# A fused layer on one core: the output projection takes the first 128 tokens' four blocks first, and two weight blocks are read twice

## The chip, the cores and the metric

The kernel runs on one core of a Trainium2 chip, in fp32. The number that counts is the device time of one execution, in microseconds. The core's engines are TensorE (PE, with the weight load beside it, PEld), VectorE (DVE), ScalarE (ACT), GpSimd (POOL) and SyncE (SP). SP and POOL issue nearly all transfers; these run on 16 DMA engines, where SP's lie in queue q1 and POOL's in queue q0.

## What is computed

One layer over 256 latent tokens of width 2048. A mixing sub-layer (Fourier groups and an SSD scan, 2048 channels together) is projected by `w_out`, normalised and added to the stream. Then comes an expert retrieval: each token scores 8 heads of keys, picks 16 experts a head, takes a dot of its row with each expert's row of `expert_u`, and adds the rows of `expert_v`, weighted by the results.

```python
y_x = jnp.concatenate([fourier_branch(...), y_x_ssm], axis=-1) @ w_out[layer]   # (256, 2048) @ (2048, 2048)
x = x + gm_x * rms_norm(y_x, g_post_mix[layer])
hx2 = modulate(rms_norm(x, g_pre_ffn[layer]), sf_x, cf_x)
# peer_ffn, for each token t of a block of 128:
q = (tb @ w_query).reshape(tbn, PEER_HEADS, PEER_KEY_DIM)     # 8 heads of 128
s1, s2 = (the halves of q) . sub_keys_1, sub_keys_2           # 128 + 128 scores a head
v1, i1 = top_k(s1, 16); v2, i2 = top_k(s2, 16)                # then top 16 of the 256 sums
act = gelu(einsum('td,thkd->thk', tb, expert_u[idx]))
out = einsum('thk,thkd->td', gate * act, expert_v[idx])
x = x + gf_x * rms_norm(out, g_post_ffn[layer])
```

## The kernel before

The 256 tokens are two tiles of 128, t = 0 and t = 1. A tile and a head are a unit, u = 8 t + h, so there are 16 units of 16 dots each; a dot number n is 16 u + j.

**Weights.** `RING` is the list of the wide weight blocks (2048 x 512, 4.19 MB each), which go in turn through two SBUF slots (`wring`). `ring_load(j)` on SP waits until the block two places earlier has been used (for the projection, by the count `wo_ps` of finished blocks) and issues four pieces of 1 MB. Entries 7 to 10 are the four column blocks of `w_out` (n = 0 to 3), entries 11 and 12 the two of `w_query`.

**Output projection.** `w_out(n, t, ...)` makes one block of the result: 16 products 128x512 into one PSUM bank, `(n % 2) * 2 + t`. `OUT_ORDER` sets the order: (0,0), (0,1), (1,0), (1,1), (2,0), (3,0), (2,1), (3,1). A block whose bank was used before waits for the evacuation by ACT (`wo_out`, count `wo_evac`), and ACT begins with these only after `tail_used` says that all late tiles are done. Late tiles (`late_tiles`) are products on DVE of the modulation vector with rows of `w_mod`, which POOL loads in 512 KB pieces into five slots; `column_sums` adds them up on PE.

**To the dots.** With all four blocks of a tile, DVE makes the new stream row (`x1_make(t)`: two passes over 128x2048), ACT squares it (`x1_norm`), and DVE makes the normalised row (`h2_make(t)`: two passes more). PE transposes it (`h2_transposes`), makes a unit's query (`query(u)`: 16 products of 128x128) and its scores (`key_scores(u)`). ACT copies these out (`q_out`, `scores_out`). DVE routes the unit: `pick_keys(u)` finds the 16 best of each half, `pick_pairs(u)` the 16 best sums and the expert indices (`idx_ready`). POOL gathers by them 128 rows of 8 KB at a time (`gather`, 1.05 MB), and DVE makes the dot (`dot(n)`).

**Slots.** The weight slots become gather slots (`uslot`, 8 of them) only when all 16 queries are done (`q_ps`). Until then the first `U_EARLY` = 20 dots go through five slots (`early`), of which the fifth is the buffer `Grow[1]`, free when `h2_make(1)` is done. In DVE's order, `x1_make(1)`, the routing of unit 0 and `h2_make(1)` stand ahead of dot 0; unit 1 is routed in halves after dots 4 and 9, unit 2 after dots 17 and 21, and so on every 12 or 13 dots. From dot 20 on (`V_POS`) half rows of `expert_v` are gathered between the dots' rows, 62 of them up to dot 130, and PE adds them up with diagonal matrices.

## Time and profile before

| | us |
|---|---|
| median of 3 runs | 1838.02 (1836.51 to 1843.12) |
| the profiled execution | 1832.72 |
| its span | 1830.9 |
| PE, DVE busy | 1457.1, 1311.3 |
| POOL, ACT busy | 891.4, 435.1 |

The profile's times are counted from the start of its span; 1.8 us of the profiled execution lie outside it. In a timeline, consecutive instructions of one kind are merged (x is their number; a product is recorded twice, so 32 are one block of the projection). In the table of windows, each engine's busy time stands with its number of instructions, and then the clock that was granted to TensorE (1.00 is 2.4 GHz, 0.50 is 1.2 GHz), the busy share of the 16 DMA engines and the bytes that they moved. In the rows of the queues, packets and MB are those that were moved inside the window. Matmul ends are modelled, and spans on POOL are rough.

### The profile page before, as it was taken

The page shows a single profiled execution, that of the slowest core. Times are in us where ns is not written, and L with a number is a line of the kernel's source. Part 1 is how long each engine was busy: PE and PEld are TensorE (multiplying, and loading weights), DVE is VectorE, ACT ScalarE, POOL GpSimd, SP SyncE. Part 2 cuts the span into 40 slices and gives each one's busy share as a digit, 9 for nine tenths or more (in the row PEclk, how much of TensorE's full clock was granted, in tenths as well). Part 3 has the DMA queues.
Part 4 walks back from the last instruction along what each step waited for, and adds up shares of the span by engine and source line. Part 5 has one row for each costly group of instructions (what it writes and reads, how often), then busy time and mean ns, then how long its engine had stood idle before and what let it go on. Part 6 is the DMA issues. An engine that isn't in the chain of part 4 may idle for free.

```text
span 1830.9 us, 13641 instructions
## 1 busy us (share of the span) xinstructions
PE 1457.1 (80%) x4521; PEld 707.6 (39%) x4521; DVE 1311.3 (72%) x1684; ACT 435.1 (24%) x1160; POOL 891.4 (49%) x666
## 2 busy tenths in 40 slices
PE   5999999999999556655655666669999999989920
PEld 3434564575459312111111233345444444433300
DVE  3128877676138999999998787898556556556699
ACT  3012211120122222121223586687100000000000
POOL 0012233211006788888777787756455554322273
PEclk9999999999999766666667898979999999999965
DMA  9999989796658999999999999979999999999997
GB/s 364 378 361 342 352 334 326 300 348 244 221 186 345 380 418 420 418 418 420 419 419 417 405 406 391 381 291 386 414 413 412 413 413 413 381 418 417 417 422 312
DMA packets 164022, 683.72 MB, mean 373 GB/s; under 512 B 16433, under 2 KB 19057, under 8 KB 120689
## 3 DMA queue, kind: packets, MB, share of 16 engines
q0 software_dynamic: 92160, 503.36, 68.4%
q1 hardware_dynamic: 71360, 176.36, 25.5%
q10 hardware_dynamic: 432, 3.15, 0.4%
q8 instruction: 36, 0.59, 0.1%
q14 instruction: 34, 0.27, 0.0%
HBM read 678.51 MB, written 4.29 MB: 373 GB/s over the span
## 4 chain that ended last, share of the span: by engine, by line
DMA 35%; PE 28%; POOL 16%; DVE 14%; issue 5%; SPq 2%; ACT 0%; DVEq 0%; POOLq 0%; ACTq 0%
DMA arena<-in_expert_v,arena 27%; POOL arena L568 16%; DMA arena<-in_expert_u,arena 6%; PE PS L1807 6%; PE PS L1666 6%; PE PS L1567 5%; DVE arena L1382 5%; DVE arena L1425 3%; PE PS L1883 2%; DVE arena L1417 2%; PE PS L1548 2%; SPq L384 1%; PE PS L1523 1%; DMA arena<-in_w_mod 1%; DMA arena<-in_w_in 1%
## 5 line engine op out<-in xcount | busy, mean ns | idle before, releaser
L1382 DVE CUSTOM_DVE_ANT_0 arena<-arena 128x2048 f32<-128x2048 f32 x256 | 578.4, 2288 | 95.4 <-DMA arena<-in_expert_u,arena 94.4
L1883 PE MATMUL PS<-arena 128*128 128x512 f32 x512 | 364.1, 851 | 242.1 <-DMA arena<-in_expert_v,arena 242.0
L568 POOL DMA_INDIRECT arena<-in_expert_v,arena x256 | 401.9, 1570 | 285.8 <-DVE arena L1425 108.7
L568 POOL DMA_INDIRECT arena<-in_expert_u,arena x256 | 393.0, 1535 | 257.6 <-DVE arena L1357 89.5
L1935 PE MATMUL PS<-arena 128*128 128x512 f32 x1024 | 452.9, 600 | 16.3 <-DMA arena<-in_expert_v 14.2
L1935 PEld LDWEIGHTS PS<-arena 128*128 128x128 f32 x1024 | 192.7, 191 | 275.8 <-issue 227.4
L1883 PEld LDWEIGHTS PS<-arena 128*128 128x128 f32 x512 | 117.0, 253 | 456.4 <-DMA arena<-in_expert_v,arena 359.7
L1425 DVE SCALAR_TENSOR_TENSOR arena<-arena 128x2048 f32<-128x2048 f32 x62 | 145.8, 2351 | 56.9 <-DMA arena<-in_expert_v,arena 54.5
L1098 DVE SCALAR_TENSOR_TENSOR arena<-arena 128x1024 f32<-128x1024 f32 x120 | 160.9, 1341 | 25.7 <-DMA arena<-in_w_mod 22.9
L498 POOL DMA_DIRECT2D arena<-in_w_mod x128 | 68.8, 539 | 211.4 <-DVE arena L1098 180.7
L952 ACT ACTIVATE arena<-arena 128x4 f32<-128x4 f32 x64 | 13.0, 203 | 587.3 <-DVE arena L1382 516.2
L1417 DVE SCALAR_TENSOR_TENSOR arena<-arena 128x1024 f32<-128x1024 f32 x63 | 80.9, 1284 | 66.3 <-DMA arena<-in_expert_v,arena 65.1
L1666 PE MATMUL PS<-arena 128*128 128x512 f32 x256 | 111.3, 593 | 0.0
L1807 PE MATMUL PS<-arena 128*128 128x512 f32 x256 | 110.9, 593 | 0.4 <-DVE arena L1276 0.4
L1567 PE MATMUL PS<-arena 128*128 128x512 f32 (+1 forms) x256 | 98.0, 541 | 0.1
L1666 PEld LDWEIGHTS PS<-arena 128*128 128x128 f32 x256 | 48.5, 190 | 60.3 <-issue 60.3
L1807 PEld LDWEIGHTS PS<-arena 128*128 128x128 f32 x256 | 48.3, 190 | 59.6 <-issue 59.6
L1567 PEld LDWEIGHTS PS<-arena 128*128 128x128 f32 x256 | 48.0, 190 | 45.6 <-issue 42.7
L1066 DVE TENSOR_TENSOR arena<-PS,arena 128x8 f32<-128x8 f32 x8 | 1.3, 166 | 89.2 <-PE PS L1533 89.2
L493 POOL MEMSET arena<- 128x1 f32 x8 | 0.3, 115 | 123.6 <-PE PS L1533 123.6
L1853 PE MATMUL PS<-arena 128*128 128x128 f32 x512 | 59.7, 275 | 0.5 <-ACT arena L845 0.5
L1853 PEld LDWEIGHTS PS<-arena 128*128 128x128 f32 x512 | 59.4, 192 | 1.4 <-issue 0.7
(247 smaller groups left out, 1330.5 us busy)
## 6 DMA issues: line engine op xcount, KB each, us to landing
arena<-in_w_mod POOLq DMA_DIRECT2D x128, 512.0 KB, 7.3
arena<-in_expert_v SPq DMA_DIRECT2D x128, 512.0 KB, 8.0
arena<-in_w_mod SPq DMA_DIRECT2D x32, 1024.0 KB, 14.3
arena<-in_w_in SPq DMA_DIRECT2D x28, 1024.0 KB, 14.4
arena<-in_w_out SPq DMA_DIRECT2D x16, 1024.0 KB, 12.9
arena<-in_w_query SPq DMA_DIRECT2D x8, 1024.0 KB, 8.5
arena<-in_x SPq DMA_DIRECT2D x4, 1024.0 KB, 6.1
arena<-cum_rows SPq DMA_DIRECT2D x4, 1024.0 KB, 10.0
```

Of the source, the lines that this page charges most:

```text
L498: nc.gpsimd.dma_start(slots[s], src).then_inc(tail_in[s], 16)
L568: nc.gpsimd.indirect_dma_start(slot, None, table, bass.IndirectOffsetOnAxis(ap=rows[:, n:n + 1], axis=0),).then_inc(arrived, 16)
L1098: ins = stt(acc, tile, s2[:, k, 0:1], acc, ALU.mult, ALU.add)
L1382: V.tensor_tensor_reduce(out=rows, in0=rows, in1=h2row[u // PH], scale=1.0, scalar=0.0, op0=ALU.mult, op1=ALU.add, accum_out=dots[:, u % B ...
L1417: ins = stt(a[:, 0:HALF], row, c, a[:, 0:HALF], ALU.mult, ALU.add)
L1425: ins = stt(a, row, c, a, ALU.mult, ALU.add)
L1567: ins = M(o, wring[j % 2][:, k, (b % 4) * P:(b % 4 + 1) * P], rhs, start=(k == 0), stop=(k == KT - 1))
L1666: ins = M(PS[:, j % 2, :], hT[:, 0, k, t * P:(t + 1) * P], wring[(R_FZ + c) % 2][:, k, :], start=(k == 0), stop=(k == KT - 1))
L1807: ins = M(PS[:, (n % 2) * 2 + t, :], cat[:, k % 8, t * P:(t + 1) * P], wring[(R_OUT + n) % 2][:, k, :], start=(start and k == ks[0]), stop ...
L1853: ins = M(PS[:, 4 + u % 2, 0:P], wring[j % 2][:, k, (h % 4) * P:(h % 4 + 1) * P], h2T[t][:, k, :], start=(k == 0), stop=(k == KT - 1))
L1883: ins = M(PS[:, b, :], diag_slot[m % DIAGS], slot[:, b * NQ:(b + 1) * NQ], start=(m == 0), stop=(m == BLK - 1))
L1935: ins = M(PS[:, 2 + 2 * blk + h, :], G[blk][:, i, :], tile[i % TILES][:, h * NQ:(h + 1) * NQ], start=(i == 0), stop=(i == NKEYS - 1))
```

## The change

`OUT_ORDER` becomes (0,0), (1,0), (2,0), (3,0), (2,1), (3,1), (0,1), (1,1). Weight blocks 0 and 1 are overwritten after the first tile's use and read again for the second, so `RING` has two entries more (11 and 12; `w_query` is now 13 and 14). Behind block (2,1), PE takes the first tile's transposes, the first query and its scores; the 128 columns of `w_query` for it are loaded by themselves (`first_query`, rows of 512 bytes, issued behind `ring_load(9)`). Their results have places of their own. DVE routes unit 0 right after `h2_make(0)`, does dots 0 to 9, and only then `x1_make(1)`, dot 10, the routing of unit 1 in one piece and `h2_make(1)`. The early slots serve 32 dots: four slots up to dot 11, five from dot 12. The half rows of `expert_v` begin at dot 40.

```diff
-U_EARLY = 20
+U_EARLY, EARLY_FEW = 32, 12
+EARLY_OF = [n % 4 if n < EARLY_FEW else (n - EARLY_FEW) % EARLY for n in range(U_EARLY)]
-V_POS = [20 + 110 * m // 62 if m < 62 else ...
+V_POS = [40 + 90 * m // 62 if m < 62 else ...
-        + [("out", n * NQ) for n in range(4)]
+        + [("out", n * NQ) for n in (0, 1, 2, 3, 0, 1)]
-OUT_ORDER = [(0, 0), (0, 1), (1, 0), (1, 1), (2, 0), (3, 0), (2, 1), (3, 1)]
+OUT_ORDER = [(0, 0), (1, 0), (2, 0), (3, 0), (2, 1), (3, 1), (0, 1), (1, 1)]
+OUT_DONE = [4, 8]
+OUT_LAST_USE = [1, 2, 5, 6, 7, 8]
-SUMS_AT = {(1, 0): 6, (1, 1): 7}
+SUMS_AT = {(1, 0): 6, (2, 0): 7}
+SECOND_X1_AFTER, SECOND_ROW_AFTER = 9, 10
...
                 if i >= R_OUT:
-                    sp.wait_ge(wo_ps, OUT_ORDER.index((i - R_OUT, 1)) + 1)
+                    sp.wait_ge(wo_ps, OUT_LAST_USE[i - R_OUT])
...
+            ring_load(R_OUT + 2)
+            sp.wait_ge(y_ps, 2)
+            sp.dma_start(first_query, w_query.rearrange("(k p) n -> p k n", p=P)[:, :, 0:P]).then_inc(mid_in, 16)
+            ring_load(R_OUT + 3)
...
+                    s = EARLY_OF[n]
+                    if s in EARLY_OF[:n]:
+                        pool.wait_ge(u_used, max(m for m in range(n) if EARLY_OF[m] == s) + 1)
+                    elif s == EARLY - 1:
                         pool.wait_ge(h2_ready, 2)
...
             pick_keys(0)
-            x1_variance(1)
             pick_pairs(0)
-            h2_make(1)
             for n in range(N_DENSE):
                 dot(n)
+                if n == SECOND_X1_AFTER:
+                    x1_make(1)
+                if n == SECOND_ROW_AFTER:
+                    x1_variance(1)
+                    pick_keys(1)
+                    pick_pairs(1)
+                    h2_make(1)
...
+                if (n, t) == (2, 1):
+                    h2_transposes(0)
+                    query(0)
+                    pe.wait_ge(keys_in, 32)
+                    key_scores(0)
```

On PE, from block (2,0) to the first query. In the kernel before (L1807 is the projection, L1841 a transpose, L1853 a query, L1864 the scores):

```order
L1807 MATMUL PS<-arena 128x512 [waits wo_evac,ring_in1]
L1807 MATMUL PS<-arena 128x512 x15
L1751 MATMUL PS<-arena 128x128 [waits vec_ready]
L1807 MATMUL PS<-arena 128x512 [waits wo_evac,ring_in0]
L1807 MATMUL PS<-arena 128x512 x15
L1807 MATMUL PS<-arena 128x512 [waits wo_evac]
...
L1841 MATMUL PS<-arena 128x128 [waits wo_evac,h2_ready]
...
L1853 MATMUL PS<-arena 128x128 [waits h2T_evac,ring_in1]
```

and from block (3,0) on in the kernel after (L1828, L1841, L1856, L1865 in the same meaning):

```order
L1828 MATMUL PS<-arena 128x512 [waits wo_evac,ring_in0]
L1828 MATMUL PS<-arena 128x512 x15
L1772 MATMUL PS<-arena 128x128 [waits vec_ready]
L1828 MATMUL PS<-arena 128x512 x16
L1841 MATMUL PS<-arena 128x128 [waits rows_evac,h2_ready]
...
L1856 MATMUL PS<-arena 128x128 [waits h2T_evac,mid_in]
...
L1865 MATMUL PS<-arena 128x256 [waits q_evac,keys_in]
L1828 MATMUL PS<-arena 128x512 x16
L1828 MATMUL PS<-arena 128x512 [waits wo_evac,ring_in1]
L1828 MATMUL PS<-arena 128x512 x15
L1828 MATMUL PS<-arena 128x512 [waits wo_evac,ring_in0]
L1828 MATMUL PS<-arena 128x512 x15
L1856 MATMUL PS<-arena 128x128 [waits ring_in1]
```

Three blocks of the second tile now stand behind the first scores; the last two of them wait for weights (`ring_in1`, `ring_in0`), and so does the second query.

On SP, the transfers behind the load of the stream rows. Before:

```order
L367 DMA arena<-in_w_out 128x4x512 [waits wo_ps]
...
L413 DMA tail_rows<-arena 32x128 [waits rows_evac]
L418 DMA arena<-tail_rows 128x2048 [waits gsq_ready,dram_out]
L453 DMA arena<-in_k1t 64x8x128 [waits keys_zero]
L454 DMA arena<-in_k2t 64x8x128
L367 DMA arena<-in_w_query 128x4x512 [waits wo_ps]
```

After:

```order
L372 DMA arena<-in_w_out 128x4x512 [waits wo_ps]
L372 DMA arena<-in_w_out 128x4x512 x3
L454 DMA arena<-in_w_query 128x16x128 [waits y_ps]
...
L418 DMA tail_rows<-arena 32x128 [waits rows_evac]
L423 DMA arena<-tail_rows 128x2048 [waits gsq_ready,dram_out]
L460 DMA arena<-in_k1t 64x8x128 [waits keys_zero]
L461 DMA arena<-in_k2t 64x8x128
...
L372 DMA arena<-in_w_out 128x4x512 [waits wo_ps]
L372 DMA arena<-in_w_out 128x4x512 x3
L372 DMA arena<-in_w_query 128x4x512 [waits wo_ps]
```

Two more blocks of `w_out` (8 pieces, shown by the last of them) stand between the keys and the two of `w_query`.

On DVE, after the dots have begun. In the kernel after, the second tile's row stands between dots 9 and 11 (L1398 is a dot, L1311 the start of `x1_make`, L1340 that of `pick_keys`, L1326 that of `h2_make`):

```order
L1398 ISA arena<-arena 128x2048 [waits early_in1]
...
L1311 TENSOR_REDUCE arena<-arena 128x1 [waits wo_evac]
...
L1315 RECIPROCAL arena<-arena 128x1 [waits grow_in,std_ready]
...
L1398 ISA arena<-arena 128x2048 [waits early_in2]
...
L1321 TENSOR_SCALAR arena<-arena 128x1 [waits ssq_ready]
L1340 MAX arena<-arena 128x8 [waits sc_evac]
...
L1326 RECIPROCAL arena<-arena 128x1 [waits std_ready]
...
L1398 ISA arena<-arena 128x2048 [waits early_in3]
```

Before, the same row was made ahead of dot 0, so that every dot from 10 on is now behind the last block of the projection and the second unit's scores.

## Rows read from the trace of the kernel before

**Rows 1.** The page: shares of the chain that ended last, and the dots' group.

```profile
DMA 35%; PE 28%; POOL 16%; DVE 14%; issue 5%; SPq 2%; ACT 0%; DVEq 0%; POOLq 0%; ACTq 0%
L1382 DVE CUSTOM_DVE_ANT_0 arena<-arena 128x2048 f32<-128x2048 f32 x256 | 578.4, 2288 | 95.4 <-DMA arena<-in_expert_u,arena 94.4
```

**Rows 2.** Windows: length; busy us (instructions) by engine; PE clock, DMA share, GB/s.

```profile
440.00:465.00 25.00, 25.00 (x59) 11.02 (x58) 18.98 (x16) 0.00 (x0) 6.05 (x12) 1.00 1.02 389
465.00:540.00 75.00, 74.90 (x211) 35.83 (x209) 11.16 (x14) 12.86 (x31) 1.80 (x1) 1.00 0.47 162
540.00:608.00 68.00, 66.57 (x561) 64.87 (x560) 60.02 (x106) 18.27 (x47) 34.25 (x18) 1.00 0.88 343
608.00:674.00 66.00, 30.62 (x38) 9.71 (x39) 63.32 (x113) 17.17 (x60) 55.33 (x36) 0.66 1.01 415
674.00:1000.00 326.00, 194.11 (x238) 61.42 (x237) 300.22 (x490) 74.36 (x229) 261.45 (x159) 0.66 1.02 419
1200.00:1250.00 50.00, 35.62 (x152) 22.43 (x152) 41.24 (x65) 39.21 (x108) 28.05 (x20) 0.76 0.77 284
```

**Rows 3.** Timeline of PE: start, length, line and operation.

```profile
431.15 34.50 PE L1807 MATMUL PS<-arena 128*128 128x512 f32 x80
...
482.71 13.98 PE L1807 MATMUL PS<-arena 128*128 128x512 f32 x32
...
496.64 41.37 PE L1807 MATMUL PS<-arena 128*128 128x512 f32 x96
537.84 2.23 PE L1841 MATMUL PS<-arena 128*128 128x128 f32 x16
...
606.29 1.23 PE L1864 MATMUL PS<-arena 128*128 128x256 f32 x4
```

**Rows 4.** Timeline of DVE: late tile, row of each tile, routing, dot 10.

```profile
464.14 1.29 DVE L1098 SCALAR_TENSOR_TENSOR arena<-arena 128x1024 f32<-128x1024 f32 x1 [0.77 <-DMA arena<-in_w_mod]
...
522.59 2.29 DVE L1314 TENSOR_TENSOR arena<-arena 128x2048 f32<-128x2048 f32 x1
...
542.59 2.29 DVE L1301 TENSOR_TENSOR arena<-arena 128x2048 f32<-128x2048 f32 x1
545.95 0.29 DVE L1325 MAX8 arena<-arena 128x8 f32<-128x128 f32 x1 [1.07 <-ACT arena L853]
...
555.74 0.17 DVE L1357 TENSOR_SCALAR arena<-arena 128x16 uint32<-128x16 uint32 x1
...
598.48 2.28 DVE L1382 CUSTOM_DVE_ANT_0 arena<-arena 128x2048 f32<-128x2048 f32 x1
...
654.06 0.16 DVE L1365 RECIPROCAL arena<-arena 128x1 f32<-128x1 f32 x1
```

**Rows 5.** Timelines of SP, POOL and DVE: weight loads, first gather, first dot.

```profile
451.95 6.92 SPq L367 DMA_DIRECT2D arena<-in_w_out  x4
524.30 16.00 SPq L367 DMA_DIRECT2D arena<-in_w_query  x8
...
556.77 2.47 POOL L568 DMA_INDIRECT arena<-in_expert_u,arena  x1 [89.48 <-DVE arena L1357]
...
563.95 2.29 DVE L1382 CUSTOM_DVE_ANT_0 arena<-arena 128x2048 f32<-128x2048 f32 x1 [3.26 <-DMA arena<-in_expert_u,arena]
```

**Rows 6.** DMA queues: packets, MB, share; first two in 456:464, others in 1660:1680.

```profile
q1 hardware_dynamic: 818, 1.64, 53.9%
q0 software_dynamic: 440, 1.59, 49.9%
...
q0 software_dynamic: 767, 5.58, 67.0%
q1 hardware_dynamic: 765, 2.75, 34.5%
```

**Rows 7.** Windows, columns as in the second group: PE's clock after a pause.

```profile
612.00:616.00 4.00, 0.00 (x0) 0.00 (x0) 3.96 (x4) 3.19 (x13) 3.39 (x3) 0.50 0.99 342
...
1204.00:1208.00 4.00, 4.00 (x9) 2.05 (x8) 1.31 (x2) 3.92 (x13) 3.19 (x3) 0.50 0.83 239
1208.00:1212.00 4.00, 4.00 (x20) 2.74 (x19) 2.99 (x5) 2.92 (x8) 1.53 (x2) 0.84 1.00 419
```

More of the change, by code:

```diff
@@ L61 @@
 V_LATE = 116
-V_POS = [20 + 110 * m // 62 if m < 62 else 130 + 57 * (m - 62) // 50 for m in range(V_EARLY)] + [187, 188, 190, 191]
+V_POS = [40 + 90 * m // 62 if m < 62 else 130 + 57 * (m - 62) // 50 for m in range(V_EARLY)] + [187, 188, 190, 191]
 V_AT = {n: [m for m in range(V_LATE) if V_POS[m] == n] for n in range(N_DENSE + 16)}
@@ L446, in _ @@
                 sp.dma_start(xrow[t], x[t * P:(t + 1) * P, :]).then_inc(row_in[t], 16)
-            for j in range(R_OUT + 2, R_QUERY):
-                ring_load(j)
+            ring_load(R_OUT + 2)
+            sp.wait_ge(y_ps, 2)
+            sp.dma_start(first_query, w_query.rearrange("(k p) n -> p k n", p=P)[:, :, 0:P]).then_inc(mid_in, 16)
+            ring_load(R_OUT + 3)
             rows_store(2, 2 * KT, 4 * KT)
@@ L454, in _ @@
             sp.dma_start(keys[64:P, :, NKEYS:2 * NKEYS], k2t).then_inc(keys_in, 16)
-            for j in range(R_QUERY, len(RING)):
+            for j in range(R_OUT + 4, len(RING)):
                 ring_load(j)
@@ L1318, in _ @@
             h2_make(0)
-            x1_make(1)
             go = chain(dve, route_step)
@@ L1809, in w_out, with h2_transposes, query, key_scores @@
                 return ins
+            def h2_transposes(t):
+                pe.wait_ge(h2_ready, t + 1)
+                for q in range(4):
+                    if t:
+                        pe.wait_ge(wo_evac, len(OUT_ORDER))
+                    elif q == 0:
+                        pe.wait_ge(rows_evac, 2)
+                    for i in range(4):
+                        k = 4 * q + i
+                        ins = nc.tensor.transpose(PS[:, 4 - 4 * t + q, i * P:(i + 1) * P], h2row[t][:, k * P:(k + 1) * P], ident)
+                    ins.then_inc(h2T_ps, 1)
+            def query(u):
+                t, h = divmod(u, PH)
+                j = R_QUERY + h // 4
+                if u:
+                    ring_wait(j)
+                else:
+                    pe.wait_ge(mid_in, 48)
+                if u >= 2:
+                    pe.wait_ge(q_evac, u - 1)
+                for k in range(KT):
+                    if h == 0 and k % 4 == 0:
+                        pe.wait_ge(h2T_evac, 4 * t + k // 4 + 1)
+                    ins = M(PS[:, 4 + u % 2, 0:P], wring[j % 2][:, k, (h % 4) * P:(h % 4 + 1) * P] if u else first_query[:, k, :], h2T[t][:, k, :],
+                            start=(k == 0), stop=(k == KT - 1))
+                ins.then_inc(q_ps, 1)
+            def key_scores(u):
+                t, h = divmod(u, PH)
+                pe.wait_ge(q_evac, u + 1)
+                if u >= 2:
+                    pe.wait_ge(sc_evac, u - 1)
+                M(PS[:, 6 + u % 2, 0:256], qT[:, h, t * P:(t + 1) * P] if u else first_qT, keys[:, h, :], start=True, stop=True).then_inc(sc_ps, 1)
             for n, t in OUT_ORDER:
-                if t == 0:
+                if (n, t) in OUT_ORDER[:4]:
                     ring_wait(R_OUT + n)
-                if n >= 2:
-                    pe.wait_ge(wo_evac, OUT_ORDER.index((n - 2, t)) + 1)
+                elif n < 2:
+                    ring_wait(R_OUT + 4 + n)
+                before = [i for i in range(OUT_ORDER.index((n, t))) if OUT_ORDER[i][1] == t and OUT_ORDER[i][0] % 2 == n % 2]
+                if before:
+                    pe.wait_ge(wo_evac, before[-1] + 1)
                 if (n, t) == (0, 0):
```

135 lines of the change are left out of this document (55 added, 80 removed).

## The prediction, as it was made before the change was run

> **What bounds the kernel now.** I read the shares of the chain first [rows 1]: no engine has half of it, so the limit differs by stage and has to be read by stage. The table of windows [rows 2] gives that. While the projection runs (465 to 540) PE is busy 74.9 of 75 us and the DMA engines only 0.47 of the time, at 162 GB/s. While the queries run (540 to 608) PE is busy 66.6 of 68 us, and the DMA engines idle 12%. From 608 on, when the weight slots have become gather slots, they are full (415, then 419 GB/s, share 1.01 to 1.02) and stay so for hundreds of us, with DVE close behind (63.3 of 66 us, then 300 of 326). Behind 608 the kernel is bound by bytes; ahead of it by PE and by the order of the steps. The gap at 1200 to 1250 (0.77) is another stage's.
>
> So two numbers decide: how far DVE has come with its dots at a given time, and how many expert bytes have landed when the full stretch begins.
>
> **The first tile comes earlier, but only a little.** A block is 16 products, 13.8 us (41.37 us are three) [rows 3]. Block (0,0) ends at 431.15 + 6.9 = 438.1, and (1,0) now follows it, to 452. Block (2,0) needs the bank of (0,0), so it needs ACT, and ACT waits for the last late tile, which DVE ended at 464.14 + 1.29 = 465.4 [rows 4]. That cover was the fourth block of before; now PE stands idle. And the tiles get later: `ring_load(9)` was issued at 451.95 [rows 5], now at 438.1, with `first_query` (1.05 MB) behind it. From 440 to 465 the queues moved 389 GB/s [rows 2], 9.7 MB, of which the weights had some 2.1 (the 1.64 MB of 456 to 464 [rows 6] and what little lay on both sides), the tiles 7.6. If tiles and weights share bytes evenly, as they did in 456 to 464 (1.59 and 1.64 MB [rows 6]), 15.2 MB have to pass before the last tile: 39 us, to 479. If tiles get two bytes for one, 11.4 MB, to 469. I take 474, the middle, since the 512-byte rows of `first_query` may yield to them. Then (2,0) starts at 475.5. After a pause the granted clock is 0.50, and it was 0.84 in the 4 us after the first 4 busy ones [rows 7], so a pause costs some 2 us more. (2,0) ends at 491.3, the column sums take 1.7, (3,0) ends at 506.9. Before, it ended at 496.64 + 13.8 = 510.4 [rows 3]. The first tile's rows are made in 14.5 us (510.4 to 522.59 + 2.29 [rows 4]), so by 521.4, while (2,1) runs to 520.8. From the start of the transposes to the first step of routing it was 545.95 - 537.84 = 8.1 us, from there to the first gather 10.8 and to the first dot 7.2 more [rows 3 to 5]. So routing starts at 529.6, the first gather at 540.3, **dot 0 at 547.5 instead of 563.95**: 16 us earlier.
>
> **What PE does then.** Block (3,1) runs from 529.2 to 543.0 and (0,1), whose weights were issued at 520.8 into empty queues, to 556.9. Block (1,1) needs entry 12, which SP may issue only when (3,1) is done, at 543.0: at the same time as the gathers begin to flow. This is the step that the forecast hangs on. Before, no 4.19 MB block ever met the gathers: the last piece of `w_query` was issued by 524.30 + 16 = 540.3, the first gather at 556.77 [rows 5].
>
> **How they share.** The trace shows two kinds of sharing [rows 6]. Where both queues were full (1660 to 1680), the 8-KB gather rows and the 4-KB tile rows went one for one: 767 packets to 765, so 5.58 MB to 2.75. Where 2-KB weight rows met 4-KB tile rows (456 to 464) it was 818 packets to 440, equal bytes, as if two 2-KB rows went in one turn. Put together: an 8-KB row for two 2-KB rows, so weights get a third of 417 GB/s, 139, and gathers 278. One for one throughout would give the weights a fifth (83), even bytes a half (208). I take the third, since it alone agrees with both rows.
>
> The Trainium skill (DMA: Bandwidth & Descriptors, section SWDGE vs HWDGE vs iDMA) says that an engine alternates between its queues at packet boundaries and that a packet is preferably at most 4096 bytes. By it two 2-KB rows make one turn, and the sum would be the same third; by the one-for-one row alone it would be the fifth. The trace agrees with the page in 456 to 464 (1.59 and 1.64 MB).
>
> With a third: from 544 on, 4.19 MB take 30 us, (1,1) starts at 576.5 after 20 us of idle PE and ends at 592.3. Ten dots need ten gathers; four slots let four more be issued, so 14 gathers (14.7 MB at 278) keep their share until 597. Entry 13 (the first of `w_query`), issued at 556.9 and queued behind 12, has 3.1 of its 4.19 MB by then and is there at 601. Entry 14, issued at 592.3, is there at 611.
>
> **What DVE does then.** `x1_make(1)` is done 7 us after (1,1) (538.0 to 542.59 + 2.29 before [rows 3, 4]): 599.3, and dot 10 at 601.6. Unit 1's scores come behind queries 1 and 2 (3.8 us each, by 16 of them and their scores in 66 us, and 2 us for the cold clock): 611.7. Routing takes 9.9 us (545.95 to 555.91 [rows 4]), `h2_make(1)` 4.7 (two passes of 2.3). So dot 11 starts at 626.3. In the kernel before all of this was done when dot 10 was: 598.48 + 2.3 = 600.8 [rows 4]. **DVE is 25.5 us behind**, although it began 16 us ahead. The rest up to dot 29 is the same work (53 us, 600.8 to 654.06 [rows 4]), DVE being the limit in both; one slot more or less costs nothing there, since a gather every 2.5 us is faster than dots with routing.
>
> **The same in bytes.** The queries end late (some 665 instead of 607.5 [rows 3]), but gather 32, the first to use a weight slot, also stands on POOL behind gather 31, which waits for dot 26: its bytes flow from 675.5. By then some 33 MB of expert rows are in. Before, 540 to 608 brought 17 MB beyond the last `w_query` bytes, and 67.5 us at 415 GB/s [rows 2] 28 more: 45 MB. The lack is 12 MB, 29 us at 418. The half rows of `expert_v` that begin at dot 40 instead of 20 are part of this lack and are paid later; that they are denser then (1.41 MB a dot, 3.4 us) keeps the bytes the limit. The 8.4 MB that are read twice cost nothing as bytes of their own stretch (0.47 busy before), only through what they hold up. 25.5 by DVE, 29 by bytes: I take **27 us**, as both were close to the limit behind 608.
>
> Sum: 1832.7 of the profiled execution + 27 = 1859.7. The median of the runs is 5.3 above that execution, so I forecast 1838 + 27 = **1865 us**.
>
> **The rivals.** (a) One for one: weights get a fifth. 14 gathers then end at 588 and entry 12 comes at 590.8, (1,1) ends at 606.6, dot 11 starts at 631.8: 5.5 us more than forecast, 1870. For it: the equal counts of 1660 to 1680; against it: 818 to 440.
> (b) Even bytes: entry 12 at 565.6, 13 at 585.7, but the gathers are slower (5 us each) and dot 9 ends at 598. Dot 11 at 621.6: 1860. For it: equal bytes of tiles and weights; against: 5.58 to 2.75.
> (c) Little is lost. Whatever the order, ten gathers and entries 12 and 13 (18.9 MB) must pass from 544 on before unit 1 can be routed: 589, with queries and scores 599, dot 11 at 614, +13. If the late tiles are hardly held up, so that (2,0) starts at 467 and needs no warming, all of it is up to 10 us earlier: +3, or 1841. Against it: in 456 to 464 the tiles did lose half of the queue.
> (d) Faster. If the loads of entries 12 and 13 are in the slots before the gathers take the queues, DVE never waits: dot 0 at 547.5, eleven dots (25 us), 5.5 for `x1_make(1)`, 9.9 and 4.7: dot 11 at 592.7, 8 us ahead of before; with the late tiles undisturbed (another 10 us) up to 18: 1820 to 1830. It decides at the landing of 13: it would need 20 MB in the 33 us up to 577, at 600 GB/s, where full queues moved 415 to 420 [rows 2]. So it needs my placing of the loads to be wrong, not only the shares.
> (e) The change does more harm than I see, for instance PE at half clock in stretches, or the broadcast `Grow[2]`, now issued behind (3,0), late for `h2_make(0)`: 10 us on top, 1875.
>
> **Chances.** The forecast's case 0.42, (a) 0.18, (b) 0.12, (c) 0.15 with half of it within 0.5%, (d) 0.08, (e) 0.05. The measurement of this kernel can tell 0.5% (9 us) from no change: faster 0.08, within 0.10, slower 0.82. The range takes in (a), (b), most of (c) and half of (e): 1843 to 1877.
>
> **What would show it.** In the profile after: PE idle ahead of (2,0), released by ACT; the first gather near 540 and dot 0 near 547; a pause of PE of some 20 us ahead of the last block, ended by the DMA of `in_w_out`, and a second one ahead of the second query; packets of q0 to q1 in that stretch at one to two (then the third), one to one (the fifth) or one to four (half); DVE waiting for ACT at `x1_make(1)` for some 10 us (dot 9 would be done by 583); full queues from about 675 on. I am wrong if block (1,1) starts before 565, or if the DMA engines are full already before 640 with gathers alone.

## The result: slower, and by more than forecast

| us | before | after |
|---|---|---|
| median (4 runs each) | 1839.68 (1836.51 to 1843.12) | 1877.99 (1874.77 to 1879.78) |
| profiled execution, span | 1832.72, 1830.9 | 1874.77, 1873.0 |

The ratio is 1.0206, with an interval of 1.018 to 1.0231: 38.3 us slower, where 27 were forecast. The two profiled executions lie 42.05 us apart. Of these, 5.2 were there before the first changed instruction: block (0,0) starts at 428.52 instead of 423.34. The code ahead of it is the same in all thirteen kernels of this document, and it starts anywhere from 423.3 (before) to 437.9 (e2 and e3), so this part is scatter of single executions. 36.9 us are left to explain. In the profile rows the times stay as they are in the trace; where the text compares places, it says so when they are counted from the start of block (0,0).

The shares of the chain after the change and the group of the dots, which answer to [rows 1]:

```profile
DMA 36%; PE 26%; POOL 14%; DVE 14%; issue 6%; ACT 2%; SPq 1%; DVEq 0%; ACTq 0%; POOLq 0%
...
L1398 DVE CUSTOM_DVE_ANT_0 arena<-arena 128x2048 f32<-128x2048 f32 x256 | 579.0, 2288 | 113.7 <-DMA arena<-in_expert_u,arena 111.4
```

They tell little: the dots wait 17 us longer for gathers in all (111.4 us instead of 94.4), and where the rest of the loss lies they do not show. The windows of after, with the columns of [rows 2]; three windows of 10 us stand behind the five:

```profile
440.00:465.00 25.00, 18.78 (x56) 9.16 (x54) 17.10 (x15) 0.00 (x0) 7.54 (x15) 0.89 0.94 352
465.00:540.00 75.00, 61.38 (x185) 31.11 (x186) 25.66 (x48) 11.51 (x26) 2.33 (x2) 0.88 0.57 198
540.00:608.00 68.00, 34.41 (x78) 15.02 (x78) 24.52 (x26) 4.30 (x10) 13.20 (x14) 0.75 0.86 339
608.00:674.00 66.00, 61.99 (x518) 60.93 (x517) 58.15 (x106) 17.32 (x42) 25.35 (x14) 0.97 0.79 302
674.00:1000.00 326.00, 162.08 (x242) 53.26 (x240) 299.64 (x489) 81.75 (x252) 270.05 (x164) 0.79 1.01 414
580.00:590.00 10.00, 0.00 (x0) 0.00 (x0) 0.04 (x2) 0.00 (x0) 0.94 (x1) 0.50 1.01 407
...
600.00:610.00 10.00, 10.00 (x40) 5.66 (x39) 0.31 (x2) 1.99 (x4) 0.00 (x0) 1.00 0.22 52
...
630.00:640.00 10.00, 10.00 (x89) 9.90 (x88) 9.97 (x9) 1.32 (x4) 3.85 (x2) 1.00 0.10 16
```

From 540 to 608 PE is busy 34.4 us instead of 66.6 and DVE 24.5 instead of 60.0. From 608 to 674 the engines make good what they missed, and now it is the DMA engines that have little to do: 302 GB/s instead of 415, and 16 GB/s from 630 to 640. PE's timeline shows the two pauses:

```profile
428.52 7.11 PE L1828 MATMUL PS<-arena 128*128 128x512 f32 x16 [0.36 <-DVE arena L1292]
...
436.33 20.77 PE L1828 MATMUL PS<-arena 128*128 128x512 f32 x48
456.94 1.84 PE L1621 MATMUL PS<-arena 128*128 128x1 f32 x16
477.61 16.77 PE L1828 MATMUL PS<-arena 128*128 128x512 f32 x32 [18.83 <-ACT arena L827]
...
530.80 27.63 PE L1828 MATMUL PS<-arena 128*128 128x512 f32 x64
592.02 15.90 PE L1828 MATMUL PS<-arena 128*128 128x512 f32 x32 [33.59 <-DMA arena<-in_w_out]
...
623.51 5.30 PE L1856 MATMUL PS<-arena 128*128 128x128 f32 x32 [4.01 <-DMA arena<-in_w_query]
...
674.45 1.23 PE L1865 MATMUL PS<-arena 128*128 128x256 f32 x4
```

Ahead of (2,0) PE stands 18.8 us, released by ACT's evacuation; ahead of the last block 33.6 us, released by the DMA of `in_w_out`. In the traces' own times the queries end at 675.7 instead of 607.5 [rows 3]. The timelines of DVE and POOL for the same stretch:

```profile
547.86 2.29 DVE L1398 CUSTOM_DVE_ANT_0 arena<-arena 128x2048 f32<-128x2048 f32 x1 [6.54 <-DMA arena<-in_expert_u,arena]
...
577.74 2.29 DVE L1398 CUSTOM_DVE_ANT_0 arena<-arena 128x2048 f32<-128x2048 f32 x1 [0.97 <-DMA arena<-in_expert_u,arena]
...
609.30 0.16 DVE L1311 TENSOR_REDUCE arena<-arena 128x1 f32<-128x4 f32 x1 [29.27 <-ACT arena L827]
...
633.29 2.28 DVE L1398 CUSTOM_DVE_ANT_0 arena<-arena 128x2048 f32<-128x2048 f32 x1
```

```profile
618.18 0.94 POOL L575 DMA_INDIRECT arena<-in_expert_u,arena  x1 [36.94 <-DVE arena L1398]
635.85 2.75 POOL L575 DMA_INDIRECT arena<-in_expert_u,arena  x1 [16.73 <-DVE arena L1398]
```

Dots 0 to 9 run from 547.9 to 580.0, then DVE waits 29.3 us for the last block; dot 10 starts at 615.6, dot 11 at 633.3. POOL issues gather 13 at 580, gather 14 only at 618 and gather 15 at 636, since the four slots come free with the dots. In 600 to 610 the weights are there and the slots are full: that is the 52 GB/s.

**The lag in dots and in bytes.** The table has, for after and for all experiments, how late a dot starts and how late the trace ends against before (both counted from their block (0,0)), and the bytes that queue q0 (POOL's, from then on all of them expert rows) moved in the 150 us from +110 to +260 us, where before moved 48.2 MB; the lack is turned into time at the 418 GB/s of full queues. The last column is the difference of the medians.

| kernel | dot 12 | 32 | 72 | 152 | 192 | end | q0 MB | lack, us | median |
|---|---|---|---|---|---|---|---|---|---|
| after | 27.4 | 29.1 | 27.1 | 40.0 | 37.0 | 36.9 | 32.7 | 37 | +38.3 |
| e1_rows_from_40 | -0.2 | -1.2 | -3.8 | 7.2 | 1.9 | 1.0 | 46.8 | 3 | +3.1 |
| e2_half_rows | 27.1 | 44.9 | 45.3 | 56.8 | 53.9 | 53.7 | 28.7 | 47 | +52.6 |
| e3_row_first | 30.2 | 32.0 | 30.1 | 40.2 | 36.4 | 36.2 | 31.8 | 39 | +39.8 |
| e4_tiles_first | 27.3 | 28.6 | 26.7 | 36.9 | 32.7 | 32.7 | 32.9 | 37 | +36.0 |
| e5_gathers_held | 32.5 | 34.4 | 32.5 | 44.8 | 39.6 | 37.7 | 30.7 | 42 | +41.8 |
| e6_one_read_twice | 11.2 | 13.1 | 12.1 | 24.8 | 24.1 | 26.1 | 39.4 | 21 | +23.3 |
| e7_20_early | 27.4 | 50.3 | 47.8 | 55.9 | 56.6 | 56.6 | 25.5 | 54 | +56.6 |
| c1_query_early | -0.7 | 11.3 | 5.7 | 6.4 | 1.1 | 1.3 | 45.8 | 6 | +6.8 |
| c2_query_early_28 | -0.8 | 18.1 | 17.3 | 17.5 | 16.7 | 18.7 | 41.3 | 17 | +18.0 |
| c3_exp_early | -0.8 | 8.9 | 8.2 | 8.3 | 2.8 | 2.3 | 45.1 | 7 | +11.2 |
| c4_dots_between | 0.5 | 2.6 | 1.4 | 1.4 | -2.5 | -0.4 | 47.7 | 1 | -0.2 |

DVE's position is the worse measure: after goes from 27 at dot 72 to 40 at dot 152, c1 from 11 at dot 32 to 1 at dot 192, and at dot 72 it misses the medians by up to 11 us. The bytes give all twelve medians within 6 us. The largest miss, e2, is one of the window: at +260 its queues were not yet full, and by +300 its lack has grown to 55 us, while after's is 37 at +260, at +300 and at +500 alike. One reservation: the ends of the traces lie up to 5 us to either side of the lack (7 in e2). c1 and c3, with lacks of 6 and 7 us, end only 1 and 2 us late, so a part of their +6.8 and +11.2 is not in what their traces show behind block (0,0), and stays open.

For after the lack of 37 splits in two, by the queues' rows of that stretch:

```profile
DMA packets 11111, 47.43 MB, mean 316 GB/s; under 512 B 718, under 2 KB 718, under 8 KB 6862
q0 software_dynamic: 4481, 32.66, 55.7%
q1 hardware_dynamic: 6624, 14.68, 26.3%
```

and of before:

```profile
DMA packets 10567, 55.96 MB, mean 373 GB/s; under 512 B 948, under 2 KB 948, under 8 KB 5176
q0 software_dynamic: 7457, 48.18, 79.7%
q1 hardware_dynamic: 3101, 7.66, 13.9%
```

All queues together moved 8.5 MB less (20 us at 418 GB/s), and of what they moved 7.0 MB more went through q1 (17 us). These are the 4.2 MB of the block that is read a second time for (1,1), and 2.8 MB of `w_query` that before had in ahead of +110. The other second reading, for (0,1), lies ahead of the stretch.

### The profile page after: what moved, and what is told of

It is laid out like the page before. It is cut to its first block, busy times and chain, and to the rows that moved or that the text cites. A ratio compares the mean times of both kernels' runs of the same rounds, so it can differ in the third digit from the quotient of the medians.

```text
span 1873.0 us, 13653 instructions
## 1 busy us (share of the span) xinstructions
PE 1431.9 (76%) x4521; PEld 703.6 (38%) x4521; DVE 1318.1 (70%) x1684; ACT 438.9 (23%) x1162; POOL 878.8 (47%) x666
## 4 chain that ended last, share of the span: by engine, by line
DMA 36%; PE 26%; POOL 14%; DVE 14%; issue 6%; ACT 2%; SPq 1%; DVEq 0%; ACTq 0%; POOLq 0%
DMA arena<-in_expert_v,arena 26%; POOL arena L575 14%; PE PS L1687 6%; PE PS L1588 5%; DMA arena<-in_expert_u,arena 5%; DVE arena L1398 5%; PE PS L1828 4%; DMA arena<-in_w_mod 3%; DVE arena L1441 3%; PE PS L1569 2%; DMA arena<-in_w_out 2%; DVE arena L1433 2%; PE PS L1911 2%; PE PS L1544 1%; PE PS L1711 1%
## 5 line engine op out<-in xcount | busy, mean ns | idle before, releaser
L1398 DVE CUSTOM_DVE_ANT_0 arena<-arena 128x2048 f32<-128x2048 f32 x256 | 579.0, 2288 | 113.7 <-DMA arena<-in_expert_u,arena 111.4
L1911 PE MATMUL PS<-arena 128*128 128x512 f32 x512 | 324.8, 769 | 254.9 <-DMA arena<-in_expert_v,arena 248.9
L575 POOL DMA_INDIRECT arena<-in_expert_u,arena x256 | 379.4, 1482 | 297.4 <-DVE arena L1398 159.5
L1963 PE MATMUL PS<-arena 128*128 128x512 f32 x1024 | 453.7, 601 | 17.7 <-DMA arena<-in_expert_v 15.9
L1963 PEld LDWEIGHTS PS<-arena 128*128 128x128 f32 x1024 | 193.7, 192 | 277.1 <-issue 233.9
L1911 PEld LDWEIGHTS PS<-arena 128*128 128x128 f32 x512 | 106.6, 230 | 439.3 <-DMA arena<-in_expert_v,arena 347.8
L1828 PE MATMUL PS<-arena 128*128 128x512 f32 x256 | 116.0, 614 | 52.8 <-DMA arena<-in_w_out 33.6
L1687 PE MATMUL PS<-arena 128*128 128x512 f32 x256 | 111.4, 593 | 0.0
L1828 PEld LDWEIGHTS PS<-arena 128*128 128x128 f32 x256 | 50.0, 198 | 114.9 <-issue 80.4
L1687 PEld LDWEIGHTS PS<-arena 128*128 128x128 f32 x256 | 48.7, 191 | 60.8 <-issue 60.8
L1588 PEld LDWEIGHTS PS<-arena 128*128 128x128 f32 x256 | 48.6, 192 | 46.5 <-issue 43.8
L1856 PE MATMUL PS<-arena 128*128 128x128 f32 x512 | 61.2, 279 | 4.0 <-DMA arena<-in_w_query 4.0
L1856 PEld LDWEIGHTS PS<-arena 128*128 128x128 f32 x512 | 60.7, 196 | 5.5 <-DMA arena<-in_w_query 4.4
L960 ACT ACTIVATE arena<-arena 128x128 f32<-128x128 f32 x128 | 44.9, 392 | 59.8 <-PE PS L1911 58.9
```

The source lines that it names most:

```text
L575: nc.gpsimd.indirect_dma_start(slot, None, table, bass.IndirectOffsetOnAxis(ap=rows[:, n:n + 1], axis=0),).then_inc(arrived, 16)
L1398: V.tensor_tensor_reduce(out=rows, in0=rows, in1=h2row[u // PH], scale=1.0, scalar=0.0, op0=ALU.mult, op1=ALU.add, accum_out=dots[:, u % B ...
L1588: ins = M(o, wring[j % 2][:, k, (b % 4) * P:(b % 4 + 1) * P], rhs, start=(k == 0), stop=(k == KT - 1))
L1687: ins = M(PS[:, j % 2, :], hT[:, 0, k, t * P:(t + 1) * P], wring[(R_FZ + c) % 2][:, k, :], start=(k == 0), stop=(k == KT - 1))
L1828: ins = M(PS[:, (n % 2) * 2 + t, :], cat[:, k % 8, t * P:(t + 1) * P], wring[(R_OUT + n) % 2][:, k, :], start=(start and k == ks[0]), stop ...
L1856: ins = M(PS[:, 4 + u % 2, 0:P], wring[j % 2][:, k, (h % 4) * P:(h % 4 + 1) * P] if u else first_query[:, k, :], h2T[t][:, k, :], start=(k ...
```

## Experiments

Kernels e1 to e4 ran on one chip with before at 1838.37; e5, e6, c1 and c2 on another with before at 1838.50; e7, c3 and c4 on a third with before at 1837.55. Differences to before are taken from the before of the same chip; after has its own, at 1839.68, so where a kernel is compared with after, its difference to before stands against after's 38.3.

### e1: half rows from dot 40, nothing else

```diff
-V_POS = [20 + 110 * m // 62 if m < 62 else ...
+V_POS = [40 + 90 * m // 62 if m < 62 else ...
```

(against the kernel before)

> The kernel before, with the half rows of expert_v beginning at dot 40 instead of 20 and denser up to dot 130, and nothing else. Theory (unpaid bytes): the order of the gathers alone costs time, because between dots 20 and 40 only one 1.05 MB row goes with each dot (2.5 us of full queues, while DVE with its routing needs 3.05), so the queues idle, and 5.8 MB of half rows (13.8 us) are still to be moved at dot 40: 6 to 11 us slower than before, in the trace as a lag that grows from dot 40 to dot 130. Rival (all is made before dot 11): no difference, under 2 us, and the growth of the lag from 34 to 42 us that the changed kernel shows between dots 72 and 152 comes from its late queries.

1841.47, ratio 1.0008 (0.9987 to 1.0029). This is the control for the growth from dot 72 to dot 152 in after. The growth is there by itself, from -3.8 to +7.2, and is given back by dot 192 (+1.9). So in this kernel the later half rows cost nothing that can be told from none (at most 5 us by the interval); they mainly move the place where the lag is seen. The theory that they cost 6 to 11 us by themselves fell. The changed kernel with its half rows from dot 20 was not run; in after the growth is of the same size (27.1 to 40.0), but less of it is given back by dot 192 (37.0).

### e2: the early rows in halves of 4 KB

```diff
-                    gather(expert_u, early[s], early_in[s], n)
+                    gather(u_half, early[s][:, 0:HALF], early_in[s], n, idx_left)
+                    gather(u_half, early[s][:, HALF:D], early_in[s], n, idx_right)
```

(against after, with the counts that follow from it)

> The changed kernel, with each of the first 32 gathers split into two of half rows (4 KB each), so that a packet of the gathers is 4 KB against 2 KB of the weights. Theory (one packet for one): packets of the two queues stay equal in number, bytes go 2 to 1, the weights of the last block land some 5 us sooner after their issue, the gathers come every 3.8 us instead of 3.25, and dot 11 starts 4 to 6 us earlier; in all 3 to 7 us faster than the changed kernel (1871 to 1875). Rival (the queues share bytes or something else than packets): packets 2 to 1 against q1 or no change in the landing, and no gain. POOL has twice as many gathers to issue (1.24 us each), which still fits into 3.8 us.

1890.94, ratio 1.0255 (1.0199 to 1.0311). This was the test of how the queues share. The same view of the queues in after (554 to 580) and in e2 (564 to 590), where both queues had work throughout; in after from 457 to 465, where the tiles' 4-KB rows met 2-KB weight rows; and in before from 458 to 462, the middle of the window that the forecast had read; one fence each:

```profile
q0 software_dynamic: 1161, 8.46, 78.7%
q1 hardware_dynamic: 1166, 2.32, 23.5%
```

```profile
q0 software_dynamic: 1858, 6.78, 65.9%
q1 hardware_dynamic: 1857, 3.69, 37.4%
```

```profile
q0 software_dynamic: 573, 2.09, 66.6%
q1 hardware_dynamic: 572, 1.14, 37.2%
```

```profile
q0 software_dynamic: 288, 1.05, 66.2%
q1 hardware_dynamic: 291, 0.57, 37.4%
```

It is one packet for one in all four, and in [rows 6] (767 to 765) too. The bytes go as the rows' sizes: 78:22 with 8-KB rows, 65:35 with 4-KB rows. The last block came sooner as it should:

```profile
588.59 15.40 PE L1835 MATMUL PS<-arena 128*128 128x512 f32 x32 [20.64 <-DMA arena<-in_w_out]
```

The pause is 20.6 instead of 33.6 us, yet dot 12 is as late as in after (27.1), because ten dots now came later (dot 0 by 3.2 us), and by dot 32 the lag has grown to 44.9. From 644.8 to 714 POOL issues the 34 gathers of dots 15 to 31 one behind the other without a pause: 4.1 us for the row of one dot, which full queues move in 2.5. The expected gain of 3 to 7 us became a loss of 14 (52.6 against 38.3): shares are settled by this run, their price is not.

### e3: the second tile's row after dots 0 and 1

```diff
-SECOND_X1_AFTER, SECOND_ROW_AFTER = 9, 10
+SECOND_X1_AFTER, SECOND_ROW_AFTER = 0, 1
```

> The changed kernel, but the second tile's row is made after dot 0 and its routing after dot 1, instead of after dots 9 and 10. Theory (the ten dots only take the queues from the weights): with four or five gathers in the way instead of 14, the last block of the projection starts some 20 us earlier, the queries end 15 to 20 us earlier, dot 11 starts within 5 us of where it does now, and the whole is 3 to 12 us faster than the changed kernel. Rival (the dots in between are worth their 23 us of DVE time): dot 11 comes 15 to 23 us later and the kernel is slower by that.

1878.17, ratio 1.0203 (1.0168 to 1.0239): 39.8 us slower than before against after's 38.3, where 3 to 12 us less than after had been expected. With only few gathers in the way the pause of the last block falls from 33.6 to 11.0 us:

```profile
578.66 16.90 PE L1828 MATMUL PS<-arena 128*128 128x512 f32 x32 [10.97 <-DMA arena<-in_w_out]
```

and the total does not move: dot 11 starts 2 us later than in after (29.5 against 27.4), within the 5 us expected. Whether PE waits and the ten dots run meanwhile, or PE runs and the dots come after, is here the same.

### e4: the late tiles ahead of the weights

```diff
             for t in range(2):
                 sp.dma_start(xrow[t], x[t * P:(t + 1) * P, :]).then_inc(row_in[t], 16)
+            sp.wait_ge(tail_used, 8 * KT - 5)
             ring_load(R_OUT + 2)
```

> The changed kernel, but SP issues the third weight block of the projection and first_query only when all but 5 late tiles are done. Theory (the weights hold up the late tiles, for which ACT and with it block (2,0) wait): the late tiles end 4 to 5 us earlier, (2,0) starts 3 to 5 us earlier unless its own weights come later, and the whole is 2 to 5 us faster than the changed kernel. Rival (the weights are late then): (2,0) waits for a DMA instead and nothing is gained, or up to 5 us are lost.

1874.34, ratio 1.0194 (1.0159 to 1.0229): 36.0 us slower than before, against after's 38.3. That is the expected 2 us less, but the two intervals overlap, so it is not shown to be a gain, and it did not come by the way that was expected. The first pause did not shrink, it changed its releaser:

```profile
478.70 15.56 PE L1829 MATMUL PS<-arena 128*128 128x512 f32 x32 [18.82 <-DMA arena<-in_w_out]
```

In after, block (2,0) waited 18.8 us for ACT and thereby for the tiles; here 18.8 us for its weights. The tiles and the block need the queues at the same time, and whichever stands behind is waited for, as the rival had it. Dot 12 is no earlier (27.3 against 27.4).

### e5: no gather until the first block of w_query is in

```diff
                 if n % TOPK == 0:
                     pool.wait_ge(idx_ready, n // TOPK + 1)
+                if n == 0:
+                    pool.wait_ge(ring_in[1], 16 * PIECES * 7)
```

> The changed kernel, but POOL issues the first gather only when the first of the two full w_query blocks (entry 13) has landed, so that the weights of the last projection block and of queries 1 to 3 meet no gathers. Theory (the loss is work that stands behind the last block of the projection; gathers and weights only trade places in full queues): the pause of PE ahead of the last block shrinks from 33.6 us to under 3 and the queries end some 30 us earlier, but dot 0 comes 25 us later, and since DVE still has eleven dots, two rows and one routing to do behind it (45 us), dot 11 starts within 8 us of where it does in the changed kernel; the whole within 10 us of it (1868 to 1888). Rival (the meeting itself is the loss): dot 11 starts 20 us or more earlier and the kernel comes back to within 10 us of the kernel before (under 1850).

1880.31, ratio 1.0234 (1.0198 to 1.027). Gathers and weights no longer meet, and the second pause is gone; PE goes through (0,1) and (1,1) with (3,1), as the first row shows, and stops later:

```profile
532.89 41.36 PE L1830 MATMUL PS<-arena 128*128 128x512 f32 x96
...
619.32 1.22 PE L1867 MATMUL PS<-arena 128*128 128x256 f32 x2 [37.93 <-ACT arena L855]
```

The pause vanished as expected, dot 11 came 5 us later than in after (within the 8 expected), and the whole stayed within 10 us of it (41.8 against 38.3). But I had expected the queries to end 30 us earlier, and counted from block (0,0) they ended 1 us earlier; and dot 0 came 34.5 us later instead of 25. The wait lies in ACT's order: ahead of the copy of the second query (`q_out(1)`) stands `y_norm(1)`, a square root whose argument DVE makes in the first steps of `x1_make(1)`, behind dot 9, and dot 9 now came late. Without that copy PE has no scores of unit 1, and the third query stands behind these:

```profile
618.90 0.20 ACT L833 ACTIVATE arena<-arena 128x1 f32<-128x1 f32 x1 [42.00 <-DVE arena L1314]
```

So the meeting of gathers and weights is not itself the loss: without it the same bytes and dots stand in a row.

### e6: one block read twice instead of two

```diff
-        + [("out", n * NQ) for n in (0, 1, 2, 3, 0, 1)]
+        + [("out", n * NQ) for n in (0, 1, 2, 3, 0)]
-OUT_ORDER = [(0, 0), (1, 0), (2, 0), (3, 0), (2, 1), (3, 1), (0, 1), (1, 1)]
+OUT_ORDER = [(0, 0), (1, 0), (1, 1), (2, 0), (3, 0), (2, 1), (3, 1), (0, 1)]
```

> The changed kernel with the projection in the order (0,0), (1,0), (1,1), (2,0), (3,0), (2,1), (3,1), (0,1): block (1,1) stands where its weights are still there, so only one block is read twice, and (1,1) covers most of PE's wait for the late tiles. Dots, routing and slots as in the changed kernel. Theory (the loss is when the last block of the projection ends, by PE's two pauses): the first pause shrinks from 18.8 us to about 5, the second vanishes, since the weights of (0,1) are issued before any gather, the last block ends some 45 us earlier, and then query 1 waits for its own weights beside the gathers instead: dot 11 12 to 18 us earlier than in the changed kernel, the whole 1855 to 1868. Rival (the ten dots and the slots are the loss): within 5 us of the changed kernel.

1861.77, ratio 1.0129 (1.0085 to 1.0173): 23.3 us slower than before against after's 38.3, so 15 to 16 us faster than after, and dot 11 16 us earlier, both as expected. Block (1,1) goes back to the place where it stood in the cover of the late tiles, and the first pause falls from 18.8 to 5.1 us; no pause stands ahead of the last block, but one ahead of the second query:

```profile
476.38 15.58 PE L1828 MATMUL PS<-arena 128*128 128x512 f32 x32 [5.10 <-ACT arena L827]
...
590.18 10.02 PE L1856 MATMUL PS<-arena 128*128 128x128 f32 x64 [34.17 <-DMA arena<-in_w_query]
```

The pause of 34 us is as long as the one in after, one block further on. What shrank is the number of blocks to load and to compute behind it: the last block of the projection ends 128.8 us behind the start of block (0,0) instead of 179.4.

### e7: 20 early dots instead of 32

```diff
-U_EARLY, EARLY_FEW = 32, 12
+U_EARLY, EARLY_FEW = 20, 12
```

> The changed kernel with 20 instead of 32 dots in the early slots (four slots up to dot 11, five then), so that gather 20 again waits for the end of the queries. Theory (what counts is the expert bytes that are in when the queues are full for good): gathers 20 to 31 move from under the queries to behind them, some 25 us of queue time are lost more, and the kernel is 18 to 28 us slower than the changed one (1896 to 1906); the 32 early dots give back that much of what the late queries cost. Rival (the lag is fixed at dot 11): within 5 us of the changed kernel.

1894.16, ratio 1.0303 (1.0263 to 1.0343): 56.6 us slower than before against after's 38.3, so 16 (by the medians) to 18 us slower than after, at or just under the 18 to 28 expected, and far from the rival's 5. Up to dot 12 nothing differs; then gather 20 waits for the last query:

```profile
678.00 0.94 POOL L575 DMA_INDIRECT arena<-in_expert_u,arena  x1 [27.46 <-PE PS L1856]
```

The twelve more early dots are the part of the change that helps, as long as the queries end that late.

### c1 and c2: the first query early, the projection's order untouched

Both have the order of blocks of before, nothing read twice, the first query and its scores between (2,1) and (3,1), unit 0 routed ahead of `x1_make(1)`, the half rows from dot 20, early slots in turns of five, and unit 1's exponentials on ACT behind the last query. The core of it against after:

```diff
-        + [("out", n * NQ) for n in (0, 1, 2, 3, 0, 1)]
+        + [("out", n * NQ) for n in range(4)]
-OUT_ORDER = [(0, 0), (1, 0), (2, 0), (3, 0), (2, 1), (3, 1), (0, 1), (1, 1)]
+OUT_ORDER = [(0, 0), (0, 1), (1, 0), (1, 1), (2, 0), (3, 0), (2, 1), (3, 1)]
             pick_pairs(0)
+            x1_make(1)
+            x1_variance(1)
+            h2_make(1)
             for n in range(N_DENSE):
                 dot(n)
-                if n == SECOND_X1_AFTER:
-                    x1_make(1)
-                if n == SECOND_ROW_AFTER:
...
```

with `U_EARLY` = 20 in c1 and 28 in c2.

> The order of the projection as in the kernel before (no block read twice), but with the changed kernel's transposes, first query and first scores between (2,1) and (3,1), and the routing of unit 0 ahead of the second tile's row; dots, slots (20 dots in five) and half rows (from dot 20) as in the kernel before. Theory: what costs in the changed kernel is the order of the blocks with the second reading, and the early first query alone is a gain: routing of unit 0 starts 13 us earlier than before, dot 0 some 4 us earlier (the second tile's row still stands ahead of it and is bound by the last block, which ends 8 us later than before), dot 11 3 to 5 us earlier, while the queries end up to 10 us later, because their second weight block meets the first gathers: between 6 us faster and 2 us slower than the kernel before. Rival (an early first query costs by itself, through the later last block): 8 us slower or more.

> The same as the run ahead of it, with 28 instead of 20 dots in the five early slots, so that POOL needs the weight slots (free when the queries end) eight dots later. Theory (the later end of the queries holds back gather 20): 1 to 4 us faster than with 20. Rival (five slots are too few once the queues could be full): 1 to 4 us slower.

c1: 1845.27, ratio 1.0037 (1.0014 to 1.0059). c2: 1856.53, ratio 1.0086 (1.005 to 1.0122). c1 is 6.8 us slower than before, between the forecast (6 us faster to 2 slower) and the rival (8 or more); its trace ends 1.3 us later. Of after's 38.3 us, 31.5 are gone. c1 differs from after in more than the reads and the order (slots, half rows, the place of the second row), so this bounds what the early first query costs and does not share out the rest. c1 loses 13 us at dot 16, where DVE waits for unit 1's exponentials, which ACT makes only behind the last query:

```profile
633.87 0.16 DVE L1381 RECIPROCAL arena<-arena 128x1 f32<-128x1 f32 x1 [12.88 <-ACT arena L842]
```

Most of it is given back by dot 192 (+1.1). More early dots do harm here: c2 is 18.0 us slower than before, 11 more than c1, where 1 to 4 faster or, by the rival, 1 to 4 slower had been expected. Its gather 21 has to go into the early slot of dot 16 and so waits for the same exponentials:

```profile
632.97 2.75 POOL L575 DMA_INDIRECT arena<-in_expert_u,arena  x1 [13.10 <-DVE arena L1399]
```

c1 waits there for the last query only, 9.1 us, and then has the eight weight slots: counted from block (0,0), its gathers 21 to 27 go out from 200.2 to 217.8, those of c2 from 204.1 to 227.2. e7 and c2 go opposite ways. In e7 the queries end 247.3 us behind the start of block (0,0), and POOL waits 27.5 us for them; in c2 they end at 198.9, ahead of the dot for whose slot POOL waits. How much of c2's loss is the late exponentials and how much the number of slots, no run takes apart.

### c3 and c4: toward a version that beats before

c3 takes the exponentials forward on ACT (`EXP_AT = 10` instead of the end). c4 has 24 early dots besides, and two dots in the waits of the second row:

```diff
-U_EARLY, EARLY_FEW = 20, 0
+U_EARLY, EARLY_FEW = 24, 0
             x1_make(1)
+            dot(0)
             x1_variance(1)
+            dot(1)
             h2_make(1)
```

(c4 against c3)

> The kernel with the first query early and no block read twice, but ACT makes unit 1's exponentials after query 10 instead of after the last query. Theory (its 12.3 us at dot 16 were DVE's wait for these, since the queries end later): the step at dot 16 vanishes, dots run 0 to 1 us ahead of the kernel before up to there, and the whole is 5 to 8 us faster than with the late exponentials, within 3 us of the kernel before. Rival (dot 16 waited for something else): no change.

> The same as the run ahead of it, with 24 dots in the early slots, and dots 0 and 1 on DVE inside the waits of the second tile's row (behind its first half and behind its variance). Theory: dot 2 comes 2 to 4 us earlier, gather 20 no longer waits for the queries, which end 13 us later than before, and expert bytes at 260 us behind the first block are 1 to 2 MB above the kernel before: 1 to 5 us faster than it. Rival (five early slots and the weights of queries 4 to 7 in the same queues eat the head start): within 2 us of the kernel before or slower.

c3: 1848.71, ratio 1.0061 (1.0036 to 1.0086): 11.2 us slower than before, where within 3 had been expected, and by the medians 4 us slower than c1 instead of 5 to 8 faster; the two traces end 2.3 and 1.3 us later than before. The step at dot 16 is gone, but dots 20 to 28 now wait for their gathers, which stand behind the last query: it ends 14 us later than in before, counted from block (0,0). c4: 1837.38, ratio 0.9999 (0.9982 to 1.0015), where 1 to 5 us faster had been expected, by 1 to 2 MB more than before; it moved 0.5 MB less. It has dot 0 9.2 us earlier than before, and at dot 12 nothing of it is left. No kernel here beats before. c4 shows that the early first query can be had for nothing; it also brings nothing, and the bytes, of which c4 lacks 1 us, agree with that.

## Why the prediction was right and where it was wrong

**What bounds the kernel**: right. The forecast named two numbers, DVE's place in the dots and the bytes landed when the full stretch begins; the table of twelve kernels shows that the second gives the time, within 6 us.

**The first pause**: right. PE stood ahead of (2,0), released by ACT. Counted from block (0,0), as all times of after in this section, (2,0) started at 472.4 (forecast 475.5), routing at 526.2 (529.6), dot 0 at 542.7 (547.5).

**"How they share"**: wrong, and the largest miss ahead of the dots. I took a third for the weights, because 818 packets stood against 440 in [rows 6]. That window was no fair one: POOL had issued its last tile at 455.84, q0 ran empty within the window, and q1 took what was left; in the middle of it, 458 to 462, it is 288 to 291. The same place in after has 573 to 572. One for one was rival (a), and the row of 1660 to 1680 had said so. Under the gathers the weights got 2.32 of 10.78 MB, a fifth. Entry 12 came not at 576.5 but at 586.8 ((a): 590.8), the last block ended at 602.7 (592.3, (a): 606.6).

The Trainium skill (DMA: Bandwidth & Descriptors, section SWDGE vs HWDGE vs iDMA) was cited for a packet of preferably at most 4096 bytes, by which two 2-KB rows would make one turn. No run agrees: 2-KB rows went one for one with 8-KB rows (1161 to 1166) and with 4-KB rows (1858 to 1857). Its other statement, that an engine alternates at packet boundaries, agrees with all of these counts.

**Dot 11**: close, 628.1 instead of 626.3, but by luck: the last block ended 10.4 us late, and from its end to dot 11 the sum gave 34.0 us where it took 25.4. By then the first block of `w_query` was in, so the pause that the forecast had ahead of the second query did not come (the rows show one of 4.0 us, ahead of the fourth). The two misses nearly cancel. DVE behind by 27.4 us was forecast as 25.5.

**"25.5 by DVE, 29 by bytes: I take 27"**: this is the step that failed. Two limits were averaged, though the sentence on bytes already said that the full queues decide. And the bytes were mis-sized. Before had 45.0 MB of q0 in by 675.5, as forecast; after had 29.7 MB at the same distance from its block (0,0), not 33. In POOL's timeline gather 30, not gather 32, is about to be issued then; gather 32 goes out at 680.4 (685.53 in the trace):

```profile
685.53 1.90 POOL L575 DMA_INDIRECT arena<-in_expert_u,arena  x1 [0.30 <-issue]
```

So the lack is 15.3 MB, 37 us at 418 GB/s, not 12 MB and 29 us. With it the same way of adding up gives 1838 + 37 = 1875; with the bytes as they had been sized, but not averaged, it gives 1867. The last queries also came late (670.5 instead of 665), but that cost nothing here: gather 32, the first that needs them, went out 10 us behind them and waited for nothing. What was short were the early slots, which came free with dots 10 to 26.

**"The 8.4 MB that are read twice cost nothing as bytes of their own stretch"**: right of entry 11 alone. Entry 12 and what it pushed back, 7.0 MB, fell into the stretch that belongs to the gathers, 17 of the 37 us.

**The half rows from dot 40**: "paid later" was right as a place (dot 72 to dot 152), and e1 shows that in the kernel before it has next to no price of its own.

**Not seen**: ACT's order. e5 showed that the ten dots ahead of `x1_make(1)` can also hold up ACT in `y_norm(1)`, and with it unit 1's scores and every query from the third on.

**The range** ended at 1877, 1 us short of the median, because it took in the shares' uncertainty on DVE's way but not on the bytes' way. That 1 us is less than the 1.7 by which before's own median lies above the 1838 that the forecast started from; the miss of 11 us in the time is clear of it. Rivals (b), (c) and (d) fell: the weights did not get half, and dot 11 came 27 us late. Rival (a) had the shares right and the time (1870) too low, as it too went by DVE. Rival (e), at 1875, was nearest in time, but its example of a late `Grow[2]` did not occur: no step of `h2_make(0)` waited for a DMA. What stays open: the 37 us by the table, the 36.9 between the traces from block (0,0) on and the 38.3 between the medians agree, but no run takes the 20 us of queues without work apart from the 17 us of weights, nor the order of the blocks from the second reading.

## What to carry to other kernels

When a later stretch runs at full queues for hundreds of us, as it did here, count the bytes that have landed where it begins, and take that lack as the price; how far an engine has come is only a proxy for it. The count is good only from the point on where the queues of both kernels are full (e2). Before a share is read from a window, see that both queues have work issued for the whole of it: a queue that is running out makes the other look favoured. Reading a block twice is free only if its bytes fall where the queues have room; here it also moved the last block, and with it dot 11 and every gather that needs the slot of a later dot.
